# An encoder layer on one core: the odd token tiles are loaded through ScalarE's queue, and the first loads are reordered

## What is computed

```python
def swiglu(h, w_gate, w_up, w_down):
    return (jax.nn.silu(h @ w_gate) * (h @ w_up)) @ w_down

x = x + 0.5 * swiglu(rmsnorm(x, norm_ffn1[l]), w_ffn1_gate[l], w_ffn1_up[l], w_ffn1_down[l])
x = x + hybrid_mixer(rmsnorm(x, norm_mix[l]), ...)
x = x + 0.5 * swiglu(rmsnorm(x, norm_ffn2[l]), w_ffn2_gate[l], w_ffn2_up[l], w_ffn2_down[l])
return rmsnorm(x, norm_final)
```

## Time and profile before

| | |
|---|---|
| median of 3 executions | 2524.55 us |
| lowest, highest | 2520.45, 2525.72 us |
| the profiled execution | 2521.63 us |
| its span in the trace | 2519.8 us |
| mean granted PE clock | 0.985 |
| busy: PE, DVE, ACT, POOL | 97%, 37%, 22%, 21% |
| read from HBM, written | 126.72 MB, 36.70 MB |

### The profile page before, as it was taken

The page is one execution under the profiler, slowest core; times in us unless marked ns, Lnnn a source line. Parts: engine busy times, 40 slices in busy tenths (PEclk is TensorE's granted clock), DMA queues, the critical chain, the costliest instruction groups (busy, mean ns, idle before and its releaser), DMA issues. The chain is left out here.

```text
span 2519.8 us, 29661 instructions
## 1 busy us (share of the span) xinstructions
PE 2437.7 (97%) x12762; PEld 2037.1 (81%) x12762; DVE 923.0 (37%) x1453; ACT 555.3 (22%) x988; POOL 524.0 (21%) x283
## 2 busy tenths in 40 slices
PE   6999999999999999799998999999999999999998
PEld 5888888888888887666677878888888888888887
DVE  5322222132212246765636755622132212221224
ACT  4111111111111135533433221311111111111112
POOL 3121111111111123422213322111111111112111
PEclk8999999999999999899999999999999999999999
DMA  4110111111111125413234562011111111111012
GB/s 152 34 59 26 42 34 50 34 34 42 42 34 38 38 73 139 152 57 118 82 115 126 173 263 99 26 34 59 34 34 42 42 34 41 35 42 50 26 34 84
DMA packets 152003, 168.62 MB, mean 67 GB/s; under 512 B 15680, under 2 KB 124224, under 8 KB 151872
## 3 DMA queue, kind: packets, MB, share of 16 engines
q1 hardware_dynamic: 141504, 145.75, 18.7%
q10 hardware_dynamic: 10368, 20.98, 2.2%
HBM read 126.72 MB, written 36.70 MB: 65 GB/s over the span
## 5 line engine op out<-in xcount | busy, mean ns | idle before, releaser
L1320 PE MATMUL ps<-h_hi,w_hi 128*128 128x512 f32 (+2 forms) x2568 | 926.0, 361 | 14.4 <-ACT q_rot L806 5.8
L1321 PE MATMUL ps<-h_lo,w_hi 128*128 128x512 f32 (+2 forms) x2568 | 916.8, 357 | 0.0
L1322 PE MATMUL ps<-h_hi,w_lo 128*128 128x512 f32 (+2 forms) x2568 | 915.5, 356 | 0.0
L596 POOL TENSOR_TENSOR w_lo<-w_raw,w_hi 128x1024 fp32r<-128x1024 f32 x159 | 383.4, 2419 | 1773.6 <-ACT w_hi L721 1773.6
L1320 PEld LDWEIGHTS ps<-h_hi,w_hi 128*128 128x128 f32 (+1 forms) x2568 | 489.5, 191 | 105.5 <-issue 22.2
L1322 PEld LDWEIGHTS ps<-h_hi,w_lo 128*128 128x128 f32 (+1 forms) x2568 | 489.4, 191 | 70.5
L1321 PEld LDWEIGHTS ps<-h_lo,w_hi 128*128 128x128 f32 (+1 forms) x2568 | 490.0, 191 | 67.4
L1070 DVE TENSOR_TENSOR prod<-silu,ps 128x256 f32<-128x256 f32 x132 | 79.1, 599 | 983.0 <-PE ps L1322 978.1
L1360 PE MATMUL ps<-w_hi,hid_hi 128*128 128x512 f32 x880 | 343.0, 390 | 0.0
L1362 PE MATMUL ps<-w_hi,hid_lo 128*128 128x512 f32 x880 | 342.4, 389 | 0.0
L1361 PE MATMUL ps<-w_lo,hid_hi 128*128 128x512 f32 x880 | 342.3, 389 | 0.0
(11 more groups left out here) (131 smaller groups left out, 1495.6 us busy)
## 6 DMA issues: line engine op xcount, KB each, us to landing
w_raw<-in_w_ffn_gate SPq DMA_DIRECT2D x44, 512.0 KB, 3.8
w_raw<-in_w_ffn_up SPq DMA_DIRECT2D x44, 512.0 KB, 3.8
w_raw<-in_w_ffn_down SPq DMA_DIRECT2D x44, 512.0 KB, 3.5
w_raw<-in_w_in SPq DMA_DIRECT2D x14, 512.0 KB, 5.0
proj<-stage ACTq DMA_DIRECT2D x24, 256.0 KB, 2.1
x_mid<-x SPq DMA_DIRECT2D x10, 512.0 KB, 2.6
x<-in_x_sample SPq DMA_DIRECT2D x8, 512.0 KB, 8.2
proj<-gla_t ACTq DMA_DIRECT2D x4, 640.0 KB, 3.0
```

The lines of the kernel that those rows point to most:

```text
L596: nc.gpsimd.tensor_tensor(w_lo[slot][:, :, :], w_raw[raw][:, :, :], w_hi[slot][:, :, :].bitcast(F32), ALU.subtract).then_inc(w_lo_ready, 1)
L1320: mm(out, hi, rhs_hi, start=first, stop=False)
L1321: mm(out, hi, rhs_lo, start=False, stop=False)
L1322: return mm(out, lo, rhs_hi, start=False, stop=last)
```

## The change

ScalarE issues the loads of x tiles 1, 3, 5, 7 and 9 as its first instructions. SP issues x 0, gain, unit 0, ident, x 2, x 4, unit 1, x 6, unit 2, x 8, and then what it did before. Buffers, semaphores and all waits stay.

```diff
             load_x(0)
             load_gain(norm_ffn1[0:1, :])
-            load_x(1)
             load_ffn1(0)
             sp.dma_start(ident[:, :], c_ident).then_inc(ident_loaded, 16)
+            for t in (2, 4):
+                load_x(t)
             load_ffn1(1)
-            for t in range(2, 6):
-                load_x(t)
+            load_x(6)
             load_ffn1(2)
-            for t in range(6, TT):
-                load_x(t)
+            load_x(8)
...
         @block.scalar
         def _(act):
+            for t in range(1, TT, 2):
+                src = x_prompt[0][P:2 * P, :] if t == 1 else x_sample[0][(t - 2) * P:(t - 1) * P, :]
+                act.dma_start(x_tile(0, t), src).then_inc(x_loaded[t], 16)
+
```

## The result

| | before | after |
|---|---|---|
| median of 12 executions each | 2524.16 us | 2530.19 us |
| lowest, highest | 2518.32, 2526.3 | 2526.34, 2535.64 |
| ratio, 95% interval | | 1.0027, 1.0018 to 1.0036 |
| profiled execution, its span | 2521.63, 2519.8 | 2530.05, 2528.2 |

The change makes the kernel slower by 0.27% by the ratio, which is +6.8 us, with +4.5 to +9.1 by its interval. Between the two medians lie +6.0 us. Forecast were +7.8 (2532.3, range 2526 to 2537).

The account below looks back on a forecast made before the run. PE is busy 97% of the span, and its start waits for the up tile's landing. Terms 0 + 0 + 7.8 + 0 gave +7.8 us on the median 2524.55, so 2532.3 us, range 2526 to 2537.

Parts of the forecast that it names:

- What bounds the start: First 16 us: PE's first products start 4.2 us after the up tile (second weight tile, w_ffn_up) lands.
- Six tiles at 1.3 us, +7.8, landing at 19.5: Load order at the start: six more 512 KB x tiles ahead of the up tile delay its landing from 11.73.
- Two queues share and don't add up: Loads at the start: SP's and ScalarE's queues share the same DMA engines, so the split itself is worth nothing.
- ScalarE's issues, 0: ScalarE's start: five issues take at most 4.75 us, covered by its wait for the up tile, so 0.
- Nothing is given back, +7.8 at the end: After PE's start: later pauses move along and no gap allows catching up, so the whole delay reaches the end.
- The clock, 0: PE's granted clock after its early pauses: taken as 0, could be 0 to +1.1 us.
- A: Rival at the start: ScalarE's tiles trickle behind SP's, up tile lands before 16.8, kernel not slower; chance 0.17.
- B: Rival at the start: two queues add up and slow clock stretches drop out, faster; chance 0.04 for over 0.2%.
- C: Rival at the start: ScalarE held by its own issues past about 16 us, +12 if until 20; chance 0.06.
- D: Rival on load order: the compiler moves issues, so the order is not the diff's, 0 us; chance 0.02.
- The signs it named: Trace signs of being right: up split about 19.5, first product near 23.7, x tiles 2 to 9 landed by 18.

Follow-up runs that it names:

- e1: All loads on SP's queue, none on ScalarE's, in the order in which the change's two queues issued them: 1.0028 against the kernel before.
- e2: The change with the up tile moved ahead of x 2 and x 4 on SP's queue: 1.0019 against the kernel before.
- e9: Kernel before, all loads on SP, with the up tile moved behind all ten x tiles: 1.0034 against the kernel before.
- e7: The change with first gate products waiting for the gate tile alone and h_hi of tiles 0 and 1 copied before the up tile's split: 1.0031 against before.
- e4: The change with ScalarE issuing x 3, 5, 7, 9 only after the gate tile's split, up tile ahead of x 2 on SP: 1.0000 against before.
- e3: Kernel before with only x tile 1 issued by ScalarE, all other loads on SP: 0.9997 against the kernel before.
- e8: Kernel before with gate products not awaiting up tile, ident before weights, x 1 on ScalarE's queue, POOL's roots of tiles 2, 3 before up-tile w_lo: 1.0001.

## Why the prediction was right, point by point

- *What bounds the start.* Right: the up tile's landing plus 4.2 us. It landed at 7.67 + 11.4 = 19.1 and PE started at 23.22, 4.15 later. In e1, e2 and e9 the distance is 4.1, 4.15 and 4.1. And it is what held PE: without it, in e7, PE started at 19.66.
- *Six tiles at 1.3 us, +7.8, landing at 19.5.* Measured 19.1, +7.3. The step per tile held (x 2 landed at 16.0, x 4 at 17.3, 1.3 apart), but the start that I carried over had holes, and a second queue filled some: 377 GB/s in 5 to 6 us where the earlier trace rows have 246. That can be the 0.4 us by which the term was too large; the same order on one queue, in e1, landed at 19.4. The size of the term is borne out by e2 and e9 too, 1.2 and 1.27 us for each tile.
- *Two queues share and don't add up.* Right in what it decided: e1 and e2. The highest rate in a single microsecond of the first 20 is 418 GB/s both before and after. The halves are not always equal, as the last section shows; that cost the gate tile and not the up tile.
- *ScalarE's issues, 0.* Right. They ended at 3.95 and the table load behind them at 5.26, and ScalarE then still waited 0.43 us for x 0. The first square is 1.1 late because x 0 landed at 5.7 instead of 4.6, with x 1 beside it on the other queue: e4, where ScalarE issues one load and waits 3.23 us, has the same start, 5.68. All this lies under the wait for the weights. The gate tile landed at 14.5, 4.8 late, within its cover until 16. `ident`, of which the prediction said nothing, landed at 14.7 instead of 9.9, and PE's transposes ended at 18.2, under the same cover; it is what e7 ran into next.
- *Nothing is given back, +7.8 at the end.* Right: +7.6 at the last restart and +8.0 near 925 us. e3 and e4, with the up tile at its old place, are at 0, and at -0.3 and -0.1 near 925 us. That +8.0 comes so near the +7.8 is in part luck: PE's start came 0.5 less late than forecast, and behind it another 0.7 was added, mostly by the clock.
- *The clock, 0.* Not 0, but on the slower side, within its bound of +1.1. The gate and up products of tokens 0 to 255, with the transposes between them, before and after (by stage):

```profile
15.90:24.95 9.05, 9.02 (x64) 9.04 (x64) 5.06 (x6) 4.96 (x9) 2.93 (x6) 0.81 1.09 360
```
```profile
23.20:32.85 9.65, 9.63 (x64) 9.62 (x64) 5.05 (x6) 5.01 (x9) 2.97 (x6) 0.75 0.30 91
```

The same 64 instructions take 0.6 us more at the lower granted clock, and by that the shift grew from 7.3 to 7.9. In e9 the same kind of shift was worth -1.9, of which 1.6 are the clock's. So the term is real, of either sign, and the trace of before doesn't show which.

- *From 8.0 near 925 us to the medians.* Here single executions part. e1 starts there where the change does, and by 1530 us it is 3.4 ahead (a product of PE starts at 1529.27 against 1532.64). Its row near 925 us, then the stretch behind it by stage, of the change and of e1, with the same number of PE's instructions:

```profile
933.70 1.09 PE L1333 MATMUL ps<-ident,xs 128*128 128x128 f32 x8 [1.36 <-DVE xs L1051]
```
```profile
934.00:1532.00 598.00, 548.90 (x3398) 431.08 (x3396) 371.63 (x638) 223.39 (x482) 171.55 (x79) 0.95 0.42 135
```
```profile
934.00:1529.00 595.00, 544.42 (x3398) 428.04 (x3396) 369.52 (x638) 223.22 (x482) 171.71 (x79) 0.96 0.42 136
```

That is the whole difference between their profiled spans (2528.2 at a mean clock of 0.984, 2524.8 at 0.988), and it arises in the mixer, far behind the edit, at a mean clock of 0.95 against 0.96. The +6.8 of the ratio, whose interval holds 8.0, is a mean over such executions. Whether the later start itself changes what the mixer takes isn't shown.
- *The rivals.* A (up tile before 16.8, not slower) fell: 19.1. It is e2, not the change, that comes near its limit. B (two queues add up) fell with the 418 GB/s, C (ScalarE held until 16 us) with the 3.95, and D with the order of the issues in the trace.
- *The signs it named.* One was wrong: x 2 to x 9 had not all landed by 18. x 6 and x 8, issued behind the up tile, landed at 20.4 and 23.6, and nothing waited for them.

## What to carry to other kernels

Before spreading loads over more queues, write down what is issued ahead of the transfer that ends the first wait, on all queues together: here each 512 KB put ahead of it cost 1.2 to 1.3 us, and moving it back while keeping both queues cost nothing. Loads that are wanted later belong behind it in time, as in e4, where the issuing engine's own work holds them back. What a change of the beginning is worth shows at one and the same instruction behind it, here to within 2 us for the clock, and less well in single spans: e1 and the change stood equal near 925 us and ended 3.4 apart. An earlier start is kept only if the next wait in the chain starts earlier too; here 1.3 us went to a root on POOL and then to DVE beside POOL.

## What the hardware showed that I had not expected

**Shares of two queues by size of packet.** While both had 4 KB packets, their bytes were about equal. With the gate tile (512 B runs) on SP's queue they were not. DMA view of the change, 4 to 7 us, then 9 to 13.5 us; columns are packets, MB, share of the engines' time:

```profile
q1 hardware_dynamic: 158, 0.58, 52.8%
q10 hardware_dynamic: 147, 0.54, 46.1%
...
q10 hardware_dynamic: 356, 1.26, 69.3%
q1 hardware_dynamic: 923, 0.47, 36.3%
```

So the gate tile took until 14.5 us; it landed at 9.7 before, and at 11.0 in e1, with the same order on one queue. The Trainium skill ("DMA: Bandwidth & Descriptors", "Queues, rings and completion order") says that an engine alternates between queues packet by packet, a packet there holding several descriptors. Here the queue with the small runs got 0.47 of 1.73 MB, and 923 entries against 356: neither equal bytes nor one for one in the packets that the trace counts. In the earlier trace rows 132 entries stood against 269 and the bytes were equal, so the shares of one pair of loads don't carry over to another. Turns of whole packets would allow that; the runs don't show what a turn holds.

**DVE beside POOL.** The scaling of an x tile takes 1.28 us, and 3.30 in e8, where POOL's w_lo of 2.34 us had started 0.13 us before it. The kernel before has the same at 35 us, and after the change the writing of `h_lo` beside w_lo is the other case:

```profile
35.11 2.38 POOL L596 TENSOR_TENSOR w_lo<-w_raw,w_hi 128x1024 fp32r<-128x1024 f32 x1
...
35.23 3.34 DVE L1047 SCALAR_TENSOR_TENSOR xs<-x,rstd,gain 128x1024 f32<-128x1024 f32 x1 [0.77 <-POOL rstd L605]
```
```profile
20.25 2.36 POOL L595 TENSOR_TENSOR w_lo<-w_raw,w_hi 128x1024 fp32r<-128x1024 f32 x1 [2.20 <-ACT w_hi L724]
...
20.68 2.48 DVE L1063 TENSOR_TENSOR h_lo<-ps,h_hi 128x512 fp32r<-128x512 f32 x4 [9.46 <-ACT h_hi L736]
```

The Trainium skill ("SBUF — State Buffer", "Who interferes with whom") says that VectorE and GpSimd share one pair of ports under an exclusive lock, and that a VectorE instruction with two SBUF inputs contends with a GpSimd instruction that reads SBUF, while one with at most one SBUF input, outside the 2-port modes, doesn't. The trace agrees: both scalings, which read x and `gain` from SBUF, end 1.1 us behind w_lo (in e8 21.92 against 20.83), and `h_lo`, which reads one input from PSUM, takes 2.48 us with w_lo beside it and without (at 29.52 after the change).
